# One gather of 8 KB rows per expert slot, with every v row scaled on ScalarE and summed on TensorE

## What is computed

```python
q = (xb @ w_q).reshape(PEER_BLOCK, PEER_HEADS, 2, PEER_DHALF)
s = jnp.einsum('nhpd,hpkd->nhpk', q, keys)
top_s, top_i = lax.top_k(s, PEER_TOPK)
cand = top_s[:, :, 0, :, None] + top_s[:, :, 1, None, :]
cand_idx = top_i[:, :, 0, :, None] * PEER_NKEYS + top_i[:, :, 1, None, :]
...
best_s, best_j = lax.top_k(cand, PEER_TOPK)
idx = jnp.take_along_axis(cand_idx, best_j, axis=-1)
gsm = jax.nn.softmax(best_s, axis=-1)
act = jax.nn.gelu(jnp.einsum('nd,nhkd->nhk', xb, expert_u[idx]))
return jnp.einsum('nhk,nhkd->nd', gsm * act, expert_v[idx])
```

## Time and profile before

| | us |
|---|---|
| median of 3 runs | 2366.75 (2360.18 to 2372.03) |
| span of the profiled execution | 2366.5 |
| TensorE busy | 1659.4 |
| VectorE busy | 1552.5 |
| GpSimd busy | 1386.6 |
| ScalarE busy | 594.8 |

### The profile page before, as it was taken

The page is one execution under the profiler, slowest core; times in us unless marked ns, Lnnn a source line. Parts: engine busy times, 40 slices in busy tenths (PEclk is TensorE's granted clock), DMA queues, the critical chain, the costliest instruction groups (busy, mean ns, idle before and its releaser), DMA issues. The chain is left out here.

```text
span 2366.5 us, 16881 instructions
## 1 busy us (share of the span) xinstructions
PE 1659.4 (70%) x4628; PEld 841.7 (36%) x4628; DVE 1552.5 (66%) x3174; ACT 594.8 (25%) x777; POOL 1386.6 (59%) x1231
## 2 busy tenths in 40 slices
PE   7999977888799999867754544555445556555545
PEld 3799863344345555523311111121111112111111
DVE  2450289989785666586777787587777556556554
ACT  1161222222642212322222222121222112221212
POOL 0000026565557776556666666766677886777784
PEclk9999998999799999887876666566666656765578
DMA  8766578999789999788988888988888988899996
GB/s 274 248 206 213 181 280 314 334 334 349 275 318 382 397 395 383 281 298 306 344 317 296 315 303 301 314 310 303 318 289 316 325 319 328 319 327 346 332 322 236
DMA packets 286556, 730.57 MB, mean 309 GB/s; under 512 B 22187, under 2 KB 135220, under 8 KB 286333
## 3 DMA queue, kind: packets, MB, share of 16 engines
q0 software_dynamic: 166032, 604.58, 70.5%
q1 hardware_dynamic: 119188, 123.91, 15.9%
q10 hardware_dynamic: 1250, 1.09, 0.2%
HBM read 726.43 MB, written 3.06 MB: 308 GB/s over the span
## 5 line engine op out<-in xcount | busy, mean ns | idle before, releaser
L689 PE MATMUL v_sum<-t_v_rows,t_ident 128*128 128x512 f32 (+1 forms) x1152 | 819.0, 853 | 649.2 <-DVE t_v_rows L1303 648.5
L479 POOL DMA_INDIRECT t_u_rows<-in_expert_u,t_step_idx x576 | 673.8, 1170 | 468.2 <-POOLq L478 336.5
L479 POOL DMA_INDIRECT t_v_rows<-in_expert_v,t_step_idx x576 | 681.7, 1184 | 178.3 <-issue 161.1
L1303 DVE SCALAR_TENSOR_TENSOR t_v_rows<-t_v_rows,t_wts 128x1024 f32<-128x1024 f32 x288 | 370.1, 1285 | 474.8 <-ACT t_v_rows L859 471.8
L689 PEld LDWEIGHTS v_sum<-t_v_rows,t_ident 128*128 128x128 f32 (+1 forms) x1152 | 266.0, 252 | 1156.5 <-DVE t_v_rows L1303 905.2
L859 ACT ACTIVATE t_v_rows<-t_v_rows,t_wts 128x1024 f32<-128x1024 f32 x288 | 330.5, 1147 | 1347.6 <-DMA t_v_rows<-in_expert_v,t_step_idx 1318.8
L601 PE MATMUL bank<-t_arena,t_weights 128*128 128x192 f32 (+1 forms) x2560 | 646.6, 411 | 8.2 <-issue 5.0
L601 PEld LDWEIGHTS bank<-t_arena,t_weights 128*128 128x128 f32 x2560 | 454.0, 192 | 205.3 <-issue 60.2
L1277 DVE CUSTOM_DVE_ANT_0 t_u_rows<-t_u_rows,t_arena 128x1024 f32<-128x1024 f32 x384 | 459.0, 1224 | 24.4 <-DMA t_u_rows<-in_expert_u,t_step_idx 20.5
L1277 DVE CUSTOM_DVE_ANT_0 t_u_rows<-t_u_rows,t_tok 128x1024 f32<-128x1024 f32 x192 | 227.9, 1222 | 10.2 <-DMA t_u_rows<-in_expert_u,t_step_idx 8.0
L470 POOL COPY t_step_idx<-t_idx 128x16 uint32<-128x16 uint32 x24 | 9.5, 421 | 308.9 <-DVEq L1263 308.8
(11 more groups left out here) (166 smaller groups left out, 910.8 us busy)
## 6 DMA issues: line engine op xcount, KB each, us to landing
t_weights<-in_w_in SPq DMA_DIRECT2D x40, 1024.0 KB, 6.0
t_weights<-in_w_ada SPq DMA_DIRECT2D x24, 1024.0 KB, 5.4
t_weights<-in_w_q SPq DMA_DIRECT2D x16, 1024.0 KB, 7.6
t_u_rows<-in_expert_u,t_step_idx POOLq DMA_INDIRECT x576, 6.2
t_v_rows<-in_expert_v,t_step_idx POOLq DMA_INDIRECT x576, 6.3
t_weights<-in_w_branch_a SPq DMA_DIRECT2D x8, 1024.0 KB, 10.5
t_weights<-in_w_branch_b SPq DMA_DIRECT2D x8, 1024.0 KB, 10.9
t_weights<-in_w_out SPq DMA_DIRECT2D x8, 1024.0 KB, 11.6
```

What stands on the lines that cost most here:

```text
L479: pool.indirect_dma_start(out=rows[:, k % slots, :], out_offset=None, in_=source, in_offset=bass.IndirectOffsetOnAxis(ap=step_idx[:, table ...
L689: nc.tensor.matmul(v_sum[0:m, half], add, row[:, half], start=False, stop=False).then_inc(v_free, 1)
L1303: V.scalar_tensor_tensor(out=two, in0=one, scalar=wts[:, k:k + 1], in1=two, op0=ALU.mult, op1=ALU.add).then_inc(paired_done, 1)
```

## The change

The host puts the two tables side by side, so that an expert is one row of 8 KB, u first. One gather per slot brings 128 such rows, 1 MB, into `uv_rows`, which has six places. Its indices are read where the choice left them, without a copy. VectorE takes the dot on the u half, in place. ScalarE then, slot by slot, takes the Gelu of that one dot, multiplies it by the softmax weight (an activation with a scale), and scales the v half by the result, in place. TensorE adds every v half to the sum: two matmuls per slot, four per pair. The place is free when TensorE has summed the row (`summed`), and the gather of the sixth slot after waits for that. The index copies, the step, the fused additions and the loops are gone: all 288 pairs stand in the list.

The places change too. No dot and only one choice stands ahead of the first pair. Eight query columns of group 0, the token rows of tile 1, the norm of group 1, two "ada" units and group 1's first columns go over places 0 to 31; the choices left of tiles 0 and 1 go over places 0 to 37; the rest of group 1's mixer, with eight query columns, over places 38 to 86. The other eight query columns go over places 96 to 111, and the choices of tiles 2 to 4 over places 94 to 259. The load of x of group 1 is issued from ScalarE's queue, behind the token rows of tile 1, instead of SyncE's. The host also lays the weights out in blocks, so that a partition's share of a block is one piece of 8 KB.

```diff
-NW, NU, NV, NBANK = 3, 4, 8, 6
-PAIRS = TOPK // 2
-PEELED = {2: 7, 3: 5, 4: 1}
-CHOICE_PLACES, DENSE_PLACES = 24, 87
+NW, NROW, NBANK, NCOL = 3, 6, 6, 16
+PAIRS_OF = tuple(8 * n for n in TILE_STEPS)
+PAIR0 = tuple(8 * n for n in STEP0)
+CHOICE_PLACES, COPY_PLACES, DENSE_PLACES = 38, 32, 87
...
     square, norm, *copied = first_units(1)
-    start += [[u] for u in queries[:5] + [key, queries[5], pair] + queries[6:8] + [number] + queries[8:10]
-              + [key1, queries[10], dot[0], queries[11], pair1, queries[12], queries[13], queries[14], queries[15],
-                 ("tok", 1, 0), square, dot[1], number1, norm, ("ada", 0, 22), dot[2], key2, ("ada", 0, 23), dot[3], pair2]]
-    s = staggered(start, lambda n, after: [])
-    steps = [(t, i) for t in group_tiles(0) for i in range(TILE_STEPS[t])]
-    places = [[] for _ in range(PAIRS * len(steps))]
-    later = [number2] + [u for t, y in ((0, 3), (1, 0), (1, 1), (1, 2), (1, 3)) for u in choice_units(t, y)]
-    deal(later, places, 0, CHOICE_PLACES)
-    spread(copied, places, 0, CHOICE_PLACES)
+    early = queries[8:] + [("tok", 1, 0), square, norm, ("ada", 0, 22), ("ada", 0, 23)] + copied
+    spread(early, places, 0, COPY_PLACES)
+    for n, unit in enumerate(choices):
+        places[n if n < 3 else 6 + (n - 3) * (CHOICE_PLACES - 6) // (len(choices) - 3)].append(unit)
...
     spread(mixer_units(1) + tail, places, CHOICE_PLACES, DENSE_PLACES)
-    deal(choice_units(2, 1), places, DENSE_PLACES - 2, len(places))
...
+    spread(queries[8:], places, PAIR0[2], PAIR0[2] + 16)
+    for t, first, last in ((2, PAIR0[2] - 2, PAIR0[3] - 24), (3, PAIR0[3] - 24, PAIR0[4] - 20), (4, PAIR0[4] - 20, PAIR0[4] + 40)):
+        deal([u for y in range(4) for u in choice_units(t, y) if (t, y) != (2, 0)], places, first, last)
+    def around(n, after):
+        t, j = pairs[n]
+        if after:
+            return [("sum", "pair", t, j)] + [("both", "final", t, 0)] * (j == PAIRS_OF[t] - 1)
+        return [("pair", "pair", t, j)] + [("both", "final", t - 1, j + 1)] * (t > 0 and j < 3)
+    s += staggered(places, around)
...
-        u_rows = sb("u_rows", [P, NU, D])
-        v_rows = sb("v_rows", [P, NV, D])
+        uv_rows = sb("uv_rows", [P, NROW, 2 * D])
...
-                    name = {"ada": "w_ada", "bb": "w_branch_b", "ba": "w_branch_a", "out": "w_out", "q": "w_q"}.get(kind, "w_in")
-                    c = (COLS.get(kind, 0) + b) * WB
-                    src = A[name][:, :, c:c + WB]
-                    dst = slot.rearrange("p (k n) -> p k n", k=KT)
+                    name = {"ada": "w_ada", "bb": "w_branch_b", "ba": "w_branch_a", "out": "w_out", "q": "w_q", "mix": "pool_mix",
+                            "rgig": "w_rgig"}.get(kind, "w_in")
+                    src, dst = A[name][COLS.get(kind, 0) + b], slot
...
-                if BLOCKS[n][0] == ("keytop", 0, 2):
-                    sp.wait_ge(ready["tok"], nth(("tok", 1, 3)))
-                    sp.dma_start(cols("x", 1), A["x_t1"]).then_inc(x_in, 16)
...
+            def fetch(t, n):
+                r = 2 * PAIR0[t] + n
+                if r >= NROW:
+                    pool.wait_ge(summed, r - NROW + 1)
                 pool.indirect_dma_start(
-                    out=rows[:, k % slots, :], out_offset=None, in_=source,
-                    in_offset=bass.IndirectOffsetOnAxis(ap=step_idx[:, table, par, k:k + 1], axis=0),
-                ).then_inc(landed[k % slots], 16)
...
+                    out=row(r), out_offset=None, in_=A["expert_uv"],
+                    in_offset=bass.IndirectOffsetOnAxis(ap=idx_of(t)[:, n:n + 1], axis=0),
+                ).then_inc(row_in[r % NROW], 16)
+            for role, kind, t, j in SCHEDULE:
+                if role == "pair":
+                    pairs_of_choice = PAIRS_OF[t] // 4
+                    if j % pairs_of_choice == 0:
+                        pool.wait_ge(idx_done, 4 * t + 1 + j // pairs_of_choice)
+                    fetch(t, 2 * j)
+                    fetch(t, 2 * j + 1)
...
-            def sum_pairs(t, number, pairs):
+            def sum_pair(t, j):
                 m = rows_of(t)
                 add = ident2[:, :] if t == 0 else ident[:, :]
-                for j in pairs:
-                    pe.wait_ge(paired_done, number * PAIRS + (j + 1))
-                    row = v_rows[:, (2 * j + 1) % NV, :]
-                    for half in (slice(0, 512), slice(512, D)):
-                        nc.tensor.matmul(v_sum[0:m, half], add, row[:, half], start=False, stop=False).then_inc(v_free, 1)
+                for r in range(2 * (PAIR0[t] + j), 2 * (PAIR0[t] + j) + 2):
+                    pe.wait_ge(scaled_done, r + 1)
+                    v = row(r)[:, D:]
+                    nc.tensor.matmul(v_sum[0:m, 0:512], add, v[:, 0:512], start=False, stop=False)
+                    nc.tensor.matmul(v_sum[0:m, 512:D], add, v[:, 512:D], start=False, stop=False).then_inc(summed, 1)
...
+                if t == 1:
+                    act.dma_start(cols("x", 1), A["x_t1"]).then_inc(x_in, 16)
...
-            def gelu(number):
-                act.wait_ge(dots_done, number + 1)
-                nc.scalar.activation(gelus[:, :], dots[:, :], ACT.Gelu_apprx_tanh).then_inc(gelu_done, 1)
-                act.wait_ge(wts_done, number + 1)
-            def scale_pair(number, j):
-                k = 2 * j + 1
-                row = v_rows[:, k % NV, :]
-                act.wait_ge(v_in[k % NV], number * (16 * TOPK // NV) + 16 * (k // NV + 1))
-                nc.scalar.activation(row, row, ACT.Copy, scale=wts[:, k:k + 1]).then_inc(scaled_done, 1)
+            def weigh(t, n):
+                r = 2 * PAIR0[t] + n
+                act.wait_ge(dot_done, r + 1)
+                nc.scalar.activation(gelus[:, col(r)], dots[:, col(r)], ACT.Gelu_apprx_tanh).then_inc(gelu_done, 1)
+                act.wait_ge(gelu_done, r + 1)
+                nc.scalar.activation(wts[:, col(r)], gelus[:, col(r)], ACT.Copy, scale=gsm_of(t)[:, n:n + 1]).then_inc(weight_done, 1)
+            def scale_row(r):
+                act.wait_ge(weight_done, r + 1)
+                v = row(r)[:, D:]
+                nc.scalar.activation(v, v, ACT.Copy, scale=wts[:, col(r)]).then_inc(scaled_done, 1)
...
-            def dot(t, number, k):
-                row = u_rows[:, k % NU, :]
-                dve.wait_ge(u_in[k % NU], number * (16 * TOPK // NU) + 16 * (k // NU + 1))
...
-                one, two = v_rows[:, k % NV, :], v_rows[:, (k + 1) % NV, :]
-                dve.wait_ge(v_in[k % NV], number * (16 * TOPK // NV) + 16 * (k // NV + 1))
-                dve.wait_ge(scaled_done, number * PAIRS + (j + 1))
-                V.scalar_tensor_tensor(out=two, in0=one, scalar=wts[:, k:k + 1], in1=two, op0=ALU.mult, op1=ALU.add).then_inc(paired_done, 1)
+            def dot(t, n):
+                r = 2 * PAIR0[t] + n
+                u = row(r)[:, 0:D]
+                dve.wait_ge(row_in[r % NROW], 16 * (r // NROW + 1))
+                V.tensor_tensor_reduce(out=u, in0=u, in1=h2_rows(t), scale=1.0, scalar=0.0, op0=ALU.mult, op1=ALU.add,
+                                       accum_out=dots[:, col(r)]).then_inc(dot_done, 1)
...
+        a = rows(a)
+        return np.ascontiguousarray(a.reshape(KT, P, a.shape[1] // WB, WB).transpose(2, 1, 0, 3).reshape(-1, P, KT * WB))
...
-        "expert_u": rows(expert_u), "expert_v": rows(expert_v),
+        "expert_uv": np.concatenate([rows(expert_u), rows(expert_v)], axis=1),
```

184 lines of the change are left out of this document (35 added, 149 removed).

## The result

The changed kernel takes 2289.7 us (median of 4 runs, 2286.7 to 2295.0), the kernel before in the same comparison 2365.95 us: a ratio of 0.968, interval 0.966 to 0.971, 76 us or 3.2% faster. Forecast were 2335 us and 1.3%. The time lies inside the forecast range, the direction is the forecast one, and the gain is 2.4 times the forecast gain.

The account below looks back on a forecast made before the run. The prediction took GpSimd, writing descriptors for 1152 gathers, to bound the gather stage, and TensorE the stages before. It summed 1154 us to pair 88, 1169 for the last 200 pairs and 14 to 2337, stated as 2335 us, range 2230 to 2430.

Parts of the forecast that it names:

- First gather at 308 us: Start of the kernel: 311 us before, less 3 us for weights loaded in 8 KB lines.
- Pair 39 after 328 us: First gather to pair 39: TensorE sets the pace, 308 us of work at 0.94 full, 328 us (308 to 347).
- Pair 88 after 518 us: Pairs 39 to 88, second mixer: 497 us of TensorE work at 0.96 full, 518 us (497 to 546).
- 2.6 us a slot: Last 200 pairs: undisturbed gather pace, taken between 2.55 and 2.90 us; 400 slots make 1040 us.
- 3 us a unit of choice: After pair 88: each of 33 VectorE choice units of 5.5 us leaves some 3 us uncovered by six slots, 99 us.
- 30 us for query columns and ends of tiles: Last 200 pairs: eight query columns overfill TensorE by 22 us, three tile ends cost some 3 us: 30 us.
- GpSimd's gathers at 0.94 us, no longer the bound: 576 gathers of 8 KB rows at 0.94 to 1.98 us each leave GpSimd under 40% busy.
- the DMA limit at 362 GB/s: Rival for the gather stage: DMA engines already at their limit, 2.90 us per slot, 2401 us in all; chance 0.10.
- the low clock: Rival: TensorE's row sums run at 1.2 GHz throughout, 3.5 us a row, 2602 us in all; chance 0.05.
- the bare blocks: Rival, after pair 88: each choice unit costs its whole 5.5 us, 2420 us in all; chance 0.13.
- The hidden case: Rival, after pair 88: six slots cover most of each choice unit, 1 us each, 2.55 us per slot, 2251 us; chance 0.10.
- the third rival: DMA engines already the limit: 2.90 us per slot, six slots cover 4.4 us of a choice unit, leaving 1.3; chance 0.10.

Follow-up runs that it names:

- e7: The changed kernel with the weights of w_ada, w_in, the branches, w_out and w_q loaded in 1 KB pieces again: 2292.7 us.
- e1: The changed kernel without the 33 units of choice of experts after pair 88 (tiles 2 to 4 reuse tile 1's indices and weights): 2205.8 us.
- e4: The changed kernel with the tables apart again, two gathers of 4 KB rows per slot into the same place, 1152 gathers: 2357.6 us.
- e8: The kernel before with one part changed: ScalarE scales both v rows of a pair, TensorE sums both, no addition on VectorE: 2284.0 us, one execution.
- e13: e8 once more, timed against the kernel before: 2283.6 us, ratio 0.964.

## Why the prediction was right in direction and wrong in size

Step by step, against the 2337 us of its sum, 48 us too many:

- *First gather at 308 us*: 310. In e7, with 1 KB pieces, it stands 1.3 us later, so the weights gave some 1 us, not 3.
- *Pair 39 after 328 us*: 334. TensorE's work was 301 us (308 forecast) at a fill of 0.90, not 0.94.
- *Pair 88 after 518 us*: 493, 25 us less. TensorE's work was 467 us, not 497, at a fill of 0.95 (0.96 forecast). One cause is the price of a row. In the second mixer two rows stand in the timeline as

```profile
656.41 1.02 PE L607 MATMUL v_sum<-t_uv_rows,t_ident 128*128 128x512 f32 x2
657.27 1.02 PE L608 MATMUL v_sum<-t_uv_rows,t_ident 128*128 128x512 f32 x2
658.12 5.32 PE L521 MATMUL bank<-t_arena,t_weights 128*128 128x384 f32 x16
```

  from start to next start 2 x 0.86 = 1.71 us, where the forecast's 1.88 contained the modelled end of the last matmul, which lies over the next one. Corrected, 429.6 - 62 x 1.71 + 49 x 3.42 = 491 us; the granted clock of 0.98 in place of 0.95 takes this to 476; the last 9 us stay unexplained.
- *2.6 us a slot*: 2.49 in e1. **This is the term that was mis-sized most**, 400 x 0.11 = 44 us; the 25 us of pairs 39 to 88 are the second. The lower bound, 2.55 us, was the best that 4 KB rows showed; e4 reaches 2.56 with them. That 8 KB rows move more bytes per second, 422 instead of 408 GB/s, no row of before could show, and a bound from rows of another packet size should not have been taken as the end of the range.
- *3 us a unit of choice*: 2.5 us (e1), 84 us for 99. *30 us for query columns and ends of tiles*: 50. These two errors nearly cancel.
- *GpSimd's gathers at 0.94 us, no longer the bound*: 1.16 us in the mean, and 29% busy, as said. *TensorE over 0.93 busy from 330 to 1150 us*: 0.90 and 0.95. *The end*, from the last sum: 13 us for 14.

These steps add up to some 57 us too many, not 48; the parts from e1 make 1130 us of the stage that took 1139, and that difference stays open.

The rivals fell: the DMA limit at 362 GB/s by the 422, the low clock by 0.92 to 0.98, the bare blocks by 2.5 us a unit. The hidden case had the right pace in part (2.55) and the wrong price of a unit (1 us). (In the third rival 5.5 - 4.4 us leaves 1.1, not 1.3; that changes its time by 7 us and nothing else.)

The larger fault is not in the sum. The forecast credited the faster gather stage to "one gather of 8 KB rows" and took 1152 gathers on GpSimd, at what they took there, as what had bound it. It had the row that speaks against this, 1.98 us for a gather beside a dot, and the 471.8 us that the fused additions wait for ScalarE, and priced neither: VectorE's loss of 370 us of additions was put down as work off the path. e8 shows that this was the path. A busy GpSimd was in part a blocked GpSimd, held up by the dots and additions of VectorE, the engine that the change relieves: in the stretch from 2000 to 2300 us that the forecast calls clean, its 190 gathers take 229 us, and at 0.94 us each they would take 179. So the step that failed is "GpSimd, writing descriptors for 1152 gathers, is the bound", with nothing put down for what VectorE's additions cost it; e13 shows in its place that taking them off VectorE is by itself worth 3.6%. In the changed kernel the side-by-side tables are needed, as two gathers in their place cost 68 us (e4), but with all else that was changed they leave it no faster than e13. It comes to the 89th pair later, at 1148 us where e8 and e13 come to it at 1123 to 1128; which part of the new order costs these 20 to 25 us was not tried.

## What to carry to other kernels

When an engine looks full, compare one instruction's time where it stands alone with its mean, and ask what runs on the neighbour in the slow ones: here taking a 1.3-us instruction per pair off VectorE sped up GpSimd's gathers and freed VectorE's queue, in all worth 3.6% without any of the larger rebuilding. A bound on transfers taken from one packet size is no bound for another. A long instruction sequence on the engine that frees buffers costs what the buffers don't cover; cutting it into pieces shorter than the slack gave 70 us for a reordering of the same instructions.

## What the runs showed of the hardware that was not expected

A gather queue of 8 KB rows moved 421 to 422 GB/s with all 16 DMA engines busy, one of 4 KB rows 408. An indirect gather of 128 rows costs GpSimd 0.94 us whether the rows have 4 or 8 KB. A gather that begins on GpSimd while VectorE runs a dot, an addition or a product of two tensors ends some 0.81 us after that instruction (456 of the 457 gathers over 1.05 us in the kernel before, all 284 in e8); beside maxima and searches it takes its 0.94 us. A fused multiply-add on VectorE for which nobody waits made the gathers on GpSimd 0.08 us slower in the mean and the kernel 68 us.
